# Order of VectorE's small steps in the differential attention stage: a block's maximum ahead of the older block's reciprocal

## The reference

```python
logits = einsum('bqmd,blmd->bmql', qb, k) + bias       # m: 16 maps, two for each head
logits = where(rel >= 0, logits, -inf)
p = softmax(logits, axis=-1).reshape(bsz, B_HEADS, 2, BLOCK_Q, L)
a = p[:, :, 0] - lam * p[:, :, 1]
o = einsum('bhql,blhe->bqhe', a, v)
```

## Time and profile before

| | |
|---|---|
| median of 3 runs | 3884.29 us (3883.88 to 3887.35) |
| the profiled execution's own time | 3887.83 us |
| its span, first to last instruction | 3886.0 us |
| busy: PE, PEld, DVE, ACT, POOL | 3448.4, 2575.8, 2143.9, 2016.0, 524.2 us |
| mean granted TensorE clock | 0.932 |
| second attention (`b_att`), from and to | about 2830 to 3596 us |

### The profile page before, as it was taken

How to read it: one execution, slowest core, us unless ns; L and a number is a source line. 1 busy time by engine, 2 the same in 40 slices (tenths; PEclk the granted TensorE clock), 3 DMA queues, 4 the chain that set the end, 5 groups by cost and what they waited for, 6 DMA issues and landing times. The chain is left out here.

```text
span 3886.0 us, 65323 instructions
## 1 busy us (share of the span) xinstructions
PE 3448.4 (89%) x18786; PEld 2575.8 (66%) x18786; DVE 2143.9 (55%) x5870; ACT 2016.0 (52%) x3490; POOL 524.2 (13%) x550
## 2 busy tenths in 40 slices
PE   6869798878999999996975999999978899889699
PEld 3746454466666666664855888889956666666587
DVE  3659799995555556554644111000077777777344
ACT  2548689965777777774224111111156666666222
POOL 2000255101111111110211111111020000000011
PEclk7989899977999999998987999999989999999799
DMA  8651677663233222324532444322142222220342
GB/s 231 181 135 33 194 224 230 182 211 103 80 83 81 79 75 81 83 76 138 173 135 93 117 122 118 92 70 68 57 127 69 72 69 72 69 69 30 134 140 98
DMA packets 428415, 436.41 MB, mean 112 GB/s; under 512 B 81697, under 2 KB 341185, under 8 KB 427457
## 3 DMA queue, kind: packets, MB, share of 16 engines
q1 hardware_dynamic: 417440, 430.93, 37.4%
q10 hardware_dynamic: 10784, 3.18, 0.8%
HBM read 271.44 MB, written 162.53 MB: 112 GB/s over the span
## 5 line engine op out<-in xcount | busy, mean ns | idle before, releaser
L1253 DVE CUSTOM_DVE_ANT_0 a_att_sb_lg<-a_att_ps_s,mask 128x512 f32<-128x512 f32 (+3 forms) x512 | 302.0, 595 | 220.5 <-PE a_att_ps_s L1144 179.6
L1150 PE MATMUL b_att_ps_s<-b_att_sb_k,b_att_sb_q 64*128 64x512 f32 (+3 forms) x1920 | 295.2, 418 | 84.7 <-DVE b_att_sb_lg L1255 64.0
L1327 ACT ACTIVATE a_att_sb_pT<-a_att_ps_t 128x512 f32<-128x512 f32 (+3 forms) x640 | 316.0, 530 | 104.2 <-PE a_att_ps_t L1163 97.3
L1319 ACT ACTIVATE b_att_sb_lg<-b_att_sb_lg,b_att_sb_negm 128x384 f32<-128x384 f32 (+15 forms) x256 | 305.6, 1198 | 122.6 <-DVE b_att_sb_negm L1261 122.5
L1319 ACT ACTIVATE a_att_sb_lg<-a_att_sb_lg,a_att_sb_negm 128x384 f32<-128x384 f32 (+15 forms) x256 | 307.3, 1200 | 77.5 <-DVE a_att_sb_negm L1261 77.5
L1163 PE MATMUL a_att_ps_t<-ident,a_att_sb_lg 128*128 128x128 f32 x2176 | 339.8, 279 | 0.0
L1255 DVE TENSOR_SCALAR_CACHE_REDUCE b_att_sb_lg<-b_att_ps_s 128x512 f32<-128x512 f32 (+3 forms) x512 | 282.8, 590 | 95.8 <-PE b_att_ps_s L1150 80.4
L1682 DVE TENSOR_SCALAR_CACHE_REDUCE mask<-scores,threshold_bits 128x384 bf16<-128x384 f32 (+8 forms) x288 | 322.5, 1186 | 1.2
L1163 PEld LDWEIGHTS a_att_ps_t<-ident,a_att_sb_lg 128*128 128x128 f32 x2176 | 248.6, 141 | 107.4 <-issue 57.2
L1143 PE MATMUL a_att_ps_s<-a_att_sb_k,a_att_sb_q 128*128 128x512 f32 (+3 forms) x640 | 287.1, 449 | 30.9 <-DVE a_att_sb_mx L1253 16.4
L1180 PE MATMUL a_att_ps_o<-a_att_sb_pT,a_att_sb_v 128*64 128x256 f32 (+1 forms) x2304 | 297.4, 377 | 0.0
(11 more groups left out here) (282 smaller groups left out, 6896.4 us busy)
## 6 DMA issues: line engine op xcount, KB each, us to landing
a_att_sb_q<-scratch_qT SPq DMA_DIRECT2D x512, 64.0 KB, 2.5
select_sb_w_gate<-in_a_w_in SPq DMA_DIRECT2D x32, 512.0 KB, 4.9
mask_sb_mod_w<-in_mod_w SPq DMA_DIRECT2D x16, 1024.0 KB, 6.6
a_att_sb_k<-scratch_kT SPq DMA_DIRECT2D x128, 128.0 KB, 2.8
b_qkgv_sb_w<-in_b_w_in SPq DMA_DIRECT2D x32, 512.0 KB, 4.8
b_att_sb_q<-scratch_qT SPq DMA_DIRECT2D x128, 128.0 KB, 2.5
b_att_sb_k<-scratch_kT SPq DMA_DIRECT2D x64, 256.0 KB, 4.0
front_sb_mod_w<-in_mod_w SPq DMA_DIRECT2D x8, 1024.0 KB, 8.5
```

What stands on the lines that cost most here:

```text
L1150: mm = nc.tensor.matmul(s_ps[:, (n + m) % SR, 0:z - a], q[rows, p // 2 % QS, x, cols], k[rows, slot, y, a:z], start=(j == 0), stop=(j == 2))
L1253: x = nc.vector.tensor_tensor_reduce(out, src, tab, 1.0, 2 * NEG, sign, ALU.max, top[:, col:col + 1])
L1319: nc.scalar.activation(buf, buf, ACT.Exp, bias=negm[:, p, m:m + 1], accum_out=sums[:, b, ds(h * M + m, 1)]).then_inc(exp_done, 1)
L1327: nc.scalar.activation(pT[:, r % 2, a:z, c:c + P], t_ps[:, n % TR, 0:z - a], ACT.Copy).then_inc(t_left, 1)
```

## The change

In `place` on VectorE, the call of `maximum(h, p)` is put ahead of the loop that calls `invert(head, x - 1)`. `invert` and `mix` keep their order to each other. With M = 1 no instruction moves.

```diff
                     for i in range(NCH[p]):
                         for m in range(M):
                             logits(h, p, i, m)
+                if h is not None:
+                    maximum(h, p)
                 if M == 2:
                     for head, x in both(h, p, before):
                         if 1 <= x <= NB:
                             invert(head, x - 1)
-                if h is not None:
-                    maximum(h, p)
                 for head, x in both(h, p, before):
                     for r in outputs_here(x):
                         output(head, r)
```

## The result

The changed kernel takes 3902.66 us in the median of 6 runs (3895.69 to 3907.09), the kernel before 3885.73 us in 6 runs beside it. The ratio is 1.0042, 95% interval 1.0029 to 1.0056: 16.3 us slower (11.3 to 21.8). The forecast was 9.6 us slower. The sign and the stage were right; the loss was 1.7 times the forecast, and one term of the sum was taken from the wrong row. By its time alone the result lies nearer to rival C (3903 us) than to the forecast (3893.9); the timelines have to tell the two apart.

A forecast was written before the change was run, and what follows sets the result against it. VectorE was taken to bound each head's first stretch in the second attention stage, TensorE the rest. 0.20 us in 6 places over 8 heads gave 9.6 us on 3884.3, forecast 3893.9 us, range 3884 to 3904.

The forecast's parts named there:

- rival C: TensorE's clock in the second attention stage: more idle time brings more stretches at 1.2 GHz, 9 us on top, 3903; chance 0.14.
- VectorE sets the pace in the first stretch, TensorE in the second, and only the first counts: Second attention stage, each head: VectorE is the limit for 38 us, TensorE for 55.7 us, where VectorE's idle time covers losses.
- The maximum gains nothing: Behind the last accumulator read: the maximum still starts 0.20 us later, gain costed at nothing, at most 0.16 us.
- Rival B: VectorE's maximum, 65 places where ScalarE waits: the reciprocal holds it; starting 0.16 us earlier saves 10.4 us, 3873.9; chance 0.05.
- Maximum to reciprocal 0.21: VectorE's small steps in a place: this distance should cost what maximum to ratio costs before the change, 0.21 us.
- Reciprocal to ratio 0.20: VectorE's small steps in a place: the two back to back cost 0.20 us, as seen once at the stage's end.
- upper bound of 0.26 a place: Added time from maximum to mix: at most 0.26 us a place, if the dependent pair costs what ratio to mix costs.
- Six places a head: Places where a later mix counts: 6 of 16, at 0.20 us each 1.2 us a head, 9.6 us over eight heads.
- No VectorE idle time in the first stretch: First stretch of a head: VectorE has no idle time to absorb the added 0.20 us a place.
- rival A: Whole change costs nothing: order does not matter or slack between engines absorbs the 0.20 us; 3884.3 us; chance 0.19.
- Place 14: Where the reciprocal waits 0.71 us for exponentials: the maximum starts up to 0.9 us earlier, but nothing is gained.
- price of 3.8 us for a long stretch at 1.2 GHz: Head 1 (97.46 us) against head 3 (93.68 us): a long low-clock stretch costs a head 3.8 us.

The follow-up runs named there:

- e1: Kernel before, with the new order only in places 2, 3, 4, 6, 7 and 8 of each head; ratio 1.0037 to the kernel before.
- e2: Kernel before, with the new order only in the other ten places (0, 1, 5, 9 to 15); ratio 1.0011 to the kernel before.
- e9: Changed kernel with both maps' row sums in tiles of their own (fixed addresses); ratio 1.0008 to the kernel before.
- e8: Kernel before, old order, with the second map's row sum in a tile of its own; ratio 1.0010 to the kernel before.
- e7: Changed kernel with the second map's row sum in a tile of its own; ratio 1.0040 to the kernel before.
- e4: Changed kernel with the first map's row sum in a tile of its own; ratio 1.0057 to the kernel before.
- e10: Kernel before, old order, with both maps' row sums in tiles of their own; ratio 0.9990 to the kernel before.

## Why the prediction was right, and what was off

- *VectorE sets the pace in the first stretch, TensorE in the second, and only the first counts*: held, by the two stretches after and by e1 against e2.
- *The maximum gains nothing*: held, 0.20 us in both kernels. Rival B, the faster side, needed under 0.1. The gap is not all of one piece, though. Where no chunk of the block is split into far and near keys (places 9, 11, 13 and 15) and in the unrolled places it is 0.12 us in both kernels. In place 8 the wait on the second semaphore has its value computed behind the wait on the first:

```profile
L1260 DVEq ALU_OP  x1: 40/40/40, 3164.7 to 3164.7; - x1
```

In place 9 this step is not there. So part of the 0.20 us looks like a register step too; no run took it out.
- *Maximum to reciprocal 0.21*: held, 0.21.
- *Reciprocal to ratio 0.20*: this is the step that failed. I took it from the stage's end, an unrolled part with fixed addresses and waits on constants; in the loop it is 0.31, since the ratio's address is computed from a register behind its wait. In the unrolled places of the changed kernel it is 0.19, close to the 0.20 of the prediction. My upper bound of 0.26 a place, built from ratio to mix, was also too low: the mix has no such address. The Trainium skill (VectorE: DVE Perf Modes, Rules for kernel authors) says of chained operations that the drain comes regardless and that their number is to be kept small, not the semaphores. Read as the prediction did, that the order costs nothing, it does not fit these short operations: in e9 the next one starts 0.11 us behind an independent operation and 0.20 behind a dependent one.
- *Six places a head*: nearer seven. Place 5 counts too: what the prediction took for a wait that hides 0.20 us is the stand behind the loop's jump, and it gave back 0.12 of 0.30 us at most. In the unrolled places (2 to 5 of head 0, 6 to 8 of head 7) the chain grew by 0.20 us, from 0.45 to 0.65. So the prediction's six places give 42 x 0.30 + 6 x 0.20 = 13.8 us, and seven give 49 x 0.30 + 7 x 0.20 = 16.1, or 15.3 with the 0.12 taken off in the loop, against 16.3 measured (11.3 to 21.8). That the sum meets the measurement this closely is in part luck, as the clock below shows.
- *No VectorE idle time in the first stretch* (against rival A): not so by the earlier trace rows: 2.7 us of 38 are idle, 1.55 of them the stand behind the jump.
- *Place 14*: as said. The maximum now starts 0.12 us behind its accumulator read and the reciprocal waits alone. VectorE's chain there is 0.40 us shorter (1.04 instead of 1.44), and ScalarE's next exponential waits for the copies in front of it as before. Nothing came of it:

```profile
3209.62 0.08 DVE L1253 DVE_READ_ACCUMULATOR2_ANT b_att_sb_mx<- 128x1 f32 x1
3209.74 0.17 DVE L1261 TENSOR_REDUCE b_att_sb_negm<-b_att_sb_mx 128x2 f32<-128x16 f32 x1
3210.10 0.16 DVE L1265 RECIPROCAL b_att_sb_rec<-sums 128x1 f32 x1 [0.19 <-ACT b_att_sb_lg L1319]
```

- *Rival C, the clock*: it may have a small part in the profiled execution. Heads 1 to 6 have 11.4 us each in the mean at 1.2 GHz instead of 9.7 (summed in steps of 1 us), and over heads 1 to 6 of all twelve profiles a head is 0.34 us longer per us at the low clock. That would be 0.6 of the 2.6 us a head. It is a correlation; no run changed the clock alone. The prediction's price of 3.8 us for a long stretch at 1.2 GHz, head 1 against head 3, holds something else as well: the stand behind the jump is 5.22 us in head 1 and 2.92 in head 3, which is 2.3 of the 3.8. Heads 1 to 6 stand 23.2 us in all before and 22.8 after, so this does not explain the loss.

## What to carry to other kernels

The cost of a short operation is its distance to the next start, and that depends on its neighbours: between two that depend on each other, something independent is free; ahead of a wait that has to be sat out anyway, a short operation is free too. So look first for a gap that is there anyway (here 0.20 us ahead of the maximum) and put the longest of the small steps into it that is ready, instead of moving the wanted result ahead of them.

In the hardware loop here, an address computed from a register was paid behind the instruction's wait. Don't take the price of a pair in the loop from an unrolled copy of it, and give tiny per-block operands an address of their own. And ask of an idle time at a loop's edge whether it is a wait at all before you count it as cover: look at the sequencer's own instructions, and at the turn in which the loop does not jump.

## What the runs showed of the hardware that was not expected

- The register step: 57 ns on the sequencer, 0.10 to 0.11 us on the chain when it stands behind a resolved wait or a maximum, nothing for the reciprocal's when the gap ahead of the maximum covers it (e8, against e7 and e9).
- VectorE stands still where its loop jumps back, ahead of place 6. In 48 of the 72 heads 1 to 6 of the twelve profiles the profile names no releaser:

```profile
3349.05 0.69 DVE L1255 TENSOR_SCALAR_CACHE_REDUCE b_att_sb_lg<-b_att_ps_s 128x512 f32<-128x512 f32 x1 [3.51 <-issue]
```

That is head 5 of the changed kernel. The idle time is between 1.4 and 4.1 us, and from the jump to the sequencer's next instruction it is 2.8 to 5.5 us; in head 7, where there is no jump back, VectorE goes on without a wait. Within a kernel, heads with a longer stand are longer (1.2 us per us, over these 72 heads). What the sequencer stands for there was not tried.
- Small stalls of VectorE sit at fixed places of a kernel and move when its instructions do: ratio to mix in place 6 is 0.47 to 0.48 us in the loop of the kernels before and after and 0.25 to 0.26 in e4, e7, e8, e9 and e10; place 3 has its 0.48 us in e4 and e7 alone.
